# A two-layer trunk in fp32: the first norm's squares added on VectorE, the filter's positions loaded apart, and y stored in four transfers

## The chip, the cores and the metric

The kernel runs on one core of one Trainium2 chip. The metric is device time in microseconds of one execution, the median of several. TensorE's clock has two levels here, 1.2 and 2.4 GHz; the profile gives the granted clock as a share of the upper one.

## What is computed

Two layers over 640 tokens (512 latent, 128 context) of width 1024. Cut to what matters here:

```python
def _rmsnorm(x, w):
    xf = x.astype(jnp.float32)
    y = xf * lax.rsqrt(jnp.mean(xf * xf, axis=-1, keepdims=True) + EPS)
    return (y * w.astype(jnp.float32)).astype(x.dtype)

def _trunk_layer(x, p, l, cond, ctx):
    mod = (cond @ p['w_ada'][l] + p['b_ada'][l]).reshape(cond.shape[0], 1, 6, D_MODEL)
    sh_a, sc_a, gt_a, sh_m, sc_m, gt_m = [mod[:, :, i] for i in range(6)]
    h = _rmsnorm(x, p['norm_mix_w'][l]) * (1.0 + sc_a) + sh_a
    mix, new_ctx = _mixer_sublayer(h, p, l, ctx)
    ...

def _hyena_filters(seq, w1, b1, w2, b2, w3, freq):
    ...
    z = jnp.concatenate([t[:, None], jnp.cos(ang), -jnp.sin(ang)], axis=-1)
    fr = freq.astype(f32)
    h = jnp.sin(fr * (z @ w1.astype(f32) + b1.astype(f32)))
    ...
```

After the two layers a last `_rmsnorm` gives y. The mixer has four branches; the one called Hyena makes its filter from the positions z, which depend on nothing, and applies it by a Fourier transform written as matmuls with tables.

## The kernel before, in words

Everything lies with features on the 128 partitions: x and h are eight chunks (`KC`) of 128 features by 640 tokens (`T`). Every weight is fp32 and comes in blocks of 128x1024 (512 KB) through a ring of four slots, `w_ring`. SP issues the loads in program order; each waits until TensorE has counted the block that had the slot before (`block_done`). ScalarE rounds each block to fp32r (`w_high`, L1744), POOL subtracts it from the weights (`w_low`, L617), and TensorE does three products of high and low parts (L808). All waits are on semaphores written out by hand, and each engine runs its own list in order.

**The start.** SP loads the condition, the first constants and x, and then 16 blocks of `w_early` (L585), in four rounds of four. From each TensorE makes a row block of the modulation: eight thin matmuls of 32 rows (L842; the trace shows two records for each, as for every fp32 matmul of this shape) into a bank of `psA` per round. After each round VectorE copies the rows (L2871), and after the fourth copy the last of four small matmuls turns them (L1688). VectorE adds the bias (`mod`, L2885) and makes the scale `mod_a` (L2157).
Beside this ScalarE squares x chunk by chunk (L1754) into h. After the second round TensorE sums the squares over features, with a matrix of ones, over all eight chunks (`first_norm_sum`, L855). ScalarE takes the root (`rs`, L1767 and L1768), and VectorE scales x into h (`scale_all`, L2181), in its order after the copy of the third round. ScalarE then modulates h (L1776) and rounds it (`h_high`, L1785).
POOL waits for 14 row blocks and issues the rest of the constants and of the parameters (L611, L612), after the 16th the tables (`dft`, L631, 3264 KB), which include the filter's positions `zf`, and then the low parts of the first two weight blocks.

**The entry of a layer.** `first_blocks` runs the first two blocks of the input projection side by side, chunk by chunk as `h_high` comes. Between the high and the low parts stands `filter_first` (L874), four matmuls from `zf`, which waits for `dft_in`. VectorE makes the argument of the sine (L2207 to L2215).

**The end.** `norm_sum(l, at_end)`, root, `scale_all` on VectorE, then ScalarE multiplies each chunk by the last norm's weight (L2146). SP waits for all eight and issues one transfer of y (L600).

The later norms already sum their squares on VectorE (L2821) and leave two chunks to TensorE.

## Time and profile before

| | us |
|---|---|
| median of 3 runs | 2883.03 |
| the three runs | 2883.03, 2883.29, 2879.55 |
| span of the profiled execution | 2881.2 |
| TensorE matmul busy | 2712.8 |
| VectorE busy | 1161.1 |
| ScalarE busy | 858.9 |
| POOL busy | 814.2 |

The profiled execution has no device time of its own beside its span; the span lies among the three runs. The span runs from the first to the last instruction. The page cuts it into 40 slices of 72 us; in the first, TensorE matmuls are busy for 5 tenths, the DMA engines for 8, and the granted clock is 8 tenths, while nearly everywhere after it TensorE is at 8 or 9 and the clock at 9 tenths or more. Shares of busy time are averages; what a stretch is limited by is read from the waits.

### The profile page before, as it was taken

The numbers are of one execution on the slowest core, as the hardware profiler recorded it, in microseconds if no ns is written. First come the engines' busy times: TensorE is split into PE (matmuls) and PEld (weight loads), VectorE is DVE, ScalarE is ACT, GpSimd is POOL, SyncE is SP. The second block draws the span as 40 slices with busy tenths as digits, with TensorE's granted clock in tenths as the row PEclk, the third lists the DMA queues.
The fourth block names the chain that finished last, engine by engine and source line by source line (L and its number), as shares of the span: only waits on it lengthen the run. The fifth ranks groups of instructions, "written<-read, shape, count | busy, mean of one in ns | idle before, by whom it ended". The sixth has DMA issues, their size and how long they took to land.

```text
span 2881.2 us, 56176 instructions
## 1 busy us (share of the span) xinstructions
PE 2712.8 (94%) x24352; PEld 2497.1 (87%) x24352; DVE 1161.1 (40%) x2008; ACT 858.9 (30%) x1326; POOL 814.2 (28%) x525
## 2 busy tenths in 40 slices
PE   5998899999999899999989988999999998999997
PEld 4888887888889899999977887888887998999997
DVE  3666614236633511111375674242565234111113
ACT  3242033333322422122341511433333224122223
POOL 1322121222233233333322311322222332333332
PEclk8999999999999999999999999999999999999999
DMA  8110011221234222222230100112222332222222
GB/s 314 45 48 14 3 46 43 94 83 69 81 108 138 101 88 96 88 96 88 96 135 23 45 4 11 58 68 83 83 81 78 131 102 74 88 95 88 96 88 81
DMA packets 56679, 234.25 MB, mean 81 GB/s; under 512 B 6640, under 2 KB 6800, under 8 KB 55296
## 3 DMA queue, kind: packets, MB, share of 16 engines
q1 hardware_dynamic: 53568, 206.67, 21.3%
q0 software_dynamic: 2880, 24.11, 2.3%
q8 instruction: 193, 3.16, 0.4%
q14 instruction: 38, 0.31, 0.0%
HBM read 221.94 MB, written 8.81 MB: 80 GB/s over the span
## 4 chain that ended last, share of the span: by engine, by line
PE 88%; DVE 6%; ACT 2%; DMA 2%; issue 2%; POOL 0%; SPq 0%; DVEq 0%; POOLq 0%; ACTq 0%
PE ps_dense L808 42%; PE ps_dense L816 15%; PE ps_aux L1457 4%; PE ps_aux L808 4%; PE ps_dense L1410 3%; PE ps_aux L1199 2%; PE ps_dense L1483 1%; PE ps_aux L1410 1%; PE ps_dense L842 1%; PE ps_aux L1185 1%; PE ps_aux L1151 1%; PE ps_dense L1471 1%; DMA w_ring<-in_w_early 1%; DVE arena L2442 1%; PE ps_aux L842 1%
## 5 line engine op out<-in xcount | busy, mean ns | idle before, releaser
L617 POOL TENSOR_TENSOR w_low<-w_ring,w_high 128x1024 fp32r<-128x1024 f32 x256 | 638.9, 2496 | 1317.8 <-ACT w_high L1744 1317.7
L808 PE MATMUL ps_dense<-h_high,w_high 128*128 128x320 f32 x1792 | 422.9, 318 | 38.3 <-ACT h_high L1785 30.4
L1744 ACT ACTIVATE w_high<-w_ring 128x1024 fp32r<-128x1024 f32 x256 | 270.6, 1057 | 553.6 <-PE ps_dense L808 352.3
L808 PE MATMUL ps_dense<-h_low,w_high 128*128 128x320 f32 x1792 | 402.8, 312 | 0.0
L808 PEld LDWEIGHTS ps_dense<-h_high,w_high 128*128 128x128 f32 x1792 | 305.7, 193 | 53.0 <-issue 37.6
L808 PEld LDWEIGHTS ps_dense<-h_low,w_high 128*128 128x128 f32 x1792 | 302.2, 191 | 0.5 <-issue 0.5
L808 PE MATMUL ps_dense<-h_high,w_low 128*128 128x320 f32 x1792 | 295.0, 312 | 0.0
L808 PEld LDWEIGHTS ps_dense<-h_high,w_low 128*128 128x128 f32 x1792 | 274.5, 191 | 0.0
L816 PE MATMUL ps_dense<-h_high,w_high 128*128 128x320 f32 x1024 | 242.5, 318 | 12.7 <-DVE rs L2633 5.8
L808 PE MATMUL ps_dense<-z_high,w_high 128*128 128x320 f32 x1024 | 235.5, 311 | 0.0
L816 PE MATMUL ps_dense<-h_high,w_low 128*128 128x320 f32 x1024 | 233.6, 309 | 0.0
L808 PE MATMUL ps_dense<-z_low,w_high 128*128 128x320 f32 x1024 | 233.3, 309 | 0.0
L816 PE MATMUL ps_dense<-h_low,w_high 128*128 128x320 f32 x1024 | 233.1, 309 | 0.0
L2774 DVE SCALAR_TENSOR_TENSOR x_res<-ps_dense,mod,x_res 128x320 f32<-128x320 f32 (+2 forms) x192 | 72.6, 434 | 342.6 <-PE ps_dense L808 342.6
L816 PEld LDWEIGHTS ps_dense<-h_high,w_high 128*128 128x128 f32 x1024 | 168.2, 189 | 20.7 <-issue 18.7
L2846 DVE CAST z_high<-flow 128x640 fp32r<-128x640 f32 x64 | 33.9, 529 | 368.2 <-ACT flow L2102 368.2
L808 PEld LDWEIGHTS ps_dense<-z_high,w_high 128*128 128x128 f32 x1024 | 170.3, 188 | 3.2 <-issue 3.2
L816 PEld LDWEIGHTS ps_dense<-h_low,w_high 128*128 128x128 f32 x1024 | 171.6, 188 | 0.0
L816 PEld LDWEIGHTS ps_dense<-h_high,w_low 128*128 128x128 f32 x1024 | 171.5, 188 | 0.0
L808 PEld LDWEIGHTS ps_dense<-z_low,w_high 128*128 128x128 f32 x1024 | 171.1, 188 | 0.0
L808 PE MATMUL ps_dense<-z_high,w_low 128*128 128x320 f32 x1024 | 160.6, 309 | 0.0
L808 PEld LDWEIGHTS ps_dense<-z_high,w_low 128*128 128x128 f32 x1024 | 152.8, 188 | 0.0
(450 smaller groups left out, 3931.1 us busy)
## 6 DMA issues: line engine op xcount, KB each, us to landing
w_ring<-in_w_mlp SPq DMA_DIRECT2D x128, 512.0 KB, 3.5
w_ring<-in_w_gate SPq DMA_DIRECT2D x64, 640.0 KB, 3.8
w_ring<-in_w_late SPq DMA_DIRECT2D x64, 512.0 KB, 4.6
w_ring<-in_w_early SPq DMA_DIRECT2D x48, 512.0 KB, 3.5
w_ring<-in_w_in SPq DMA_DIRECT2D x48, 512.0 KB, 3.5
w_ring<-in_w_out SPq DMA_DIRECT2D x16, 512.0 KB, 3.5
arena<-in_dft POOLq DMA_DIRECT2D x2, 3264.0 KB, 16.4
x_kept<-x_res POOLq DMA_DIRECT2D x2, 2560.0 KB, 12.9
```

The source lines that it names most:

```text
L617: g.tensor_tensor(w_low[:, n % 2], ring[:, slot, 0:KC, :], w_high[:, n % 2].bitcast(F32), ALU.subtract).then_inc(w_low_in.sem, 1)
L808: last = mm(out[:, s, 0:HALF], w_[:, par_, k, :], x_[:, k, s * HALF:(s + 1) * HALF], start=first, stop=final)
L816: last = mm(out[:, s, 0:HALF], w_[:, par_, k, :], x_[:, k, s * HALF:(s + 1) * HALF], start=k == 0 and x_ is x_high and w_ is w_high, stop= ...
L842: last = mm(out[32 * (k % 4):32 * (k % 4) + 32], cond_pad[:, k, at:at + 32], ring[:, slot, k, :], start=j == 0 and k < 4, stop=j == of - 1 ...
L1151: return mm(psA[to, 2 * i, u * 64:(u + 1) * 64], lt[s % 3][rows(r), d, hh, rows(r)], mv, start=True, stop=True)
L1185: return mm(psA[rows(r), 2 * i, u * 64:(u + 1) * 64], xt[i][at, u], wm[i][at, u], start=True, stop=True)
L1199: last = mm(out, wm[i][at, u], mv, start=not moved, stop=True)
L1410: last = mm(out[:, s, 0:HALF], w_[:, k, :], x_[:, k, s * HALF:(s + 1) * HALF], start=n == 0 and k == 0, stop=n == 2 and k == 1)
L1457: last = mm(out[:, a:b], qt, k[:, a:b], start=True, stop=True)
L1744: a(w_high[:, n % 2], ring[:, j, 0:KC, :], ACT.Copy).then_inc(w_high_in.sem, 1)
L2774: last = v.scalar_tensor_tensor(out=dst[:, p:q], in0=ps, scalar=gate[:, s:s + 1], in1=dst[:, p:q], op0=ALU.mult, op1=ALU.add)
L2846: v.tensor_copy(z_high[:, j], hid_sq[:, j % 2]).then_inc(hid_high.sem, 1)
```

## The change

Six edits:

1. `first_norm_sum` is one chunk. VectorE adds the squares of chunk c−1 to those of chunk c, for c from 1 to 7, each addition waiting for ScalarE's square and for the addition before; `squares_summed` counts them, and TensorE waits for seven.
2. TensorE does this sum after the second block of the second round, where before it did it after the fourth.
3. VectorE scales x after the copy of the second round, before the third.
4. The positions have a transfer of their own. In layer 0 POOL issues it right after the first part of the parameters, in layer 1 ahead of the tables. `filter_first` waits for that alone; the tables are waited for by VectorE before the first window product, after the fourth convolution.
5. In layer 0 the low parts of the first two weight blocks are made in four pieces of two chunks each.
6. At the end VectorE multiplies by the weight and the root in one step (`scalar_tensor_tensor`), ScalarE's part is gone, and SP issues four transfers of two chunks each.

```diff
         squares_in = signal("squares_summed", 2 * (KC - 2), KC - 1)
...
-            sp.wait_ge(y_ready.sem, KC)
-            sp.dma_start(outs["y"], h[:]).then_inc(y_out.sem, 16)
-            sp.wait_ge(y_out.sem, 16)
+            for c in range(0, KC, 2):
+                sp.wait_ge(*x_scaled.nth(DEPTH, c + 2))
+                sp.dma_start(outs["y"][:, c:c + 2], h[:, c:c + 2]).then_inc(y_out.sem, 16)
+            sp.wait_ge(y_out.sem, KC // 2 * 16)
...
             pool.dma_start(par[:, 0:PAR_FIRST], ins["par"][DEPTH - 1][:, 0:PAR_FIRST]).then_inc(params_in.sem, 16)
+            pool.dma_start(zf, ins["dft"][0:33, at_z:DFT_W]).then_inc(z_in.sem, 16)
             held(pool, block_done.sem, RING + N_EARLY - 2)
...
-                g.tensor_tensor(w_low[:, n % 2], ring[:, slot, 0:KC, :], w_high[:, n % 2].bitcast(F32),
-                                ALU.subtract).then_inc(w_low_in.sem, 1)
+                step = 2 if l == 0 and n < 2 else KC
+                for k in range(0, KC, step):
+                    last = g.tensor_tensor(w_low[:, n % 2, k:k + step], ring[:, slot, k:k + step, :],
+                                           w_high[:, n % 2, k:k + step].bitcast(F32), ALU.subtract)
+                last.then_inc(w_low_in.sem, 1)
...
-                pool.dma_start(dft, ins["dft"]).then_inc(dft_in.sem, 16)
+                if l:
+                    pool.dma_start(zf, ins["dft"][0:33, at_z:DFT_W]).then_inc(z_in.sem, 16)
+                pool.dma_start(dft[:, 0:at_z], ins["dft"][:, 0:at_z]).then_inc(dft_in.sem, 16)
...
             def first_norm_sum():
-                for c in range(KC):
-                    pe.wait_ge(*x_squared.nth(0, c + 1))
-                    for a, b in SEGS:
-                        last = mm(psD[:, 0, a:b], c_("ones"), h[:, c, a:b], start=c == 0, stop=c == KC - 1)
+                pe.wait_ge(squares_in.sem, KC - 1)
+                for a, b in SEGS:
+                    last = mm(psD[:, 0, a:b], c_("ones"), h[:, KC - 1, a:b], start=True, stop=True)
...
-                pe.wait_ge(*dft_in.nth(l, 1))
+                pe.wait_ge(*z_in.nth(l, 1))
...
-                if i == 1:
-                    pe.wait_ge(const_in.sem, 16)
-                    first_norm_sum()
+                    if i == 1 and j == 1:
+                        pe.wait_ge(const_in.sem, 16)
+                        first_norm_sum()
...
-            for c in range(KC):
-                act.wait_ge(*x_scaled.nth(DEPTH, c + 1))
-                a(h[:, c], h[:, c], ACT.Identity, scale=c_("fin")[:, c:c + 1]).then_inc(y_ready.sem, 1)
...
                 if l == DEPTH:
-                    scale_all()
+                    for c in range(KC):
+                        v.scalar_tensor_tensor(out=h[:, c], in0=x[:, c], scalar=c_("fin")[:, c:c + 1], in1=rs[:],
+                                               op0=ALU.mult, op1=ALU.mult).then_inc(x_scaled.sem, 1)
                     return
...
-                dve.wait_ge(*dft_in.nth(l, 1))
                 sin_arg(l, 1, flat, p_("hb1", r), r)
...
                         dve.wait_ge(*x_out.nth(l, 1))
+                        dve.wait_ge(*dft_in.nth(l, 1))
...
+            for c in range(1, KC):
+                dve.wait_ge(*x_squared.nth(0, c + 1))
+                if c > 1:
+                    dve.wait_ge(squares_in.sem, c - 1)
+                v.tensor_tensor(h[:, c], h[:, c], h[:, c - 1], ALU.add).then_inc(squares_in.sem, 1)
             for i in range(N_EARLY // RING):
                 dve.wait_ge(block_done.sem, RING + (i + 1) * RING)
                 v.tensor_copy(first_rows[:, i * P:(i + 1) * P], psA[:, i, 0:P]).then_inc(first_rows_in.sem, 1)
-                if i == 2:
+                if i == 1:
```

How the order moves on TensorE at the start: a row block is eight of the matmuls into `ps_aux`, and the sum is the pairs into `ps_dense` from `h_norm` (640 tokens, in 512 and 128). Before, the end of the eight pairs and what follows; the first eight row blocks (64 matmuls) stand ahead of them:

```order
L855 MATMUL ps_dense<-h_norm,con 128x512
L855 MATMUL ps_dense<-h_norm,con 128x128
L842 MATMUL ps_aux<-w_ring,cond_pad 32x128 x64
L1688 MATMUL ps_aux<-con,bout 128x8 x4
L808 MATMUL ps_dense<-h_high,w_high 128x320 x2
```

Now, from the first matmul on:

```order
L851 MATMUL ps_aux<-w_ring,cond_pad 32x128 x48
L863 MATMUL ps_dense<-h_norm,con 128x512
L863 MATMUL ps_dense<-h_norm,con 128x128
L851 MATMUL ps_aux<-w_ring,cond_pad 32x128 x80
L1696 MATMUL ps_aux<-con,bout 128x8 x4
L817 MATMUL ps_dense<-h_high,w_high 128x320 x2
```

One pair is left of eight, and it stands behind six row blocks (48 matmuls) and ahead of ten (80), where the eight pairs stood behind eight and ahead of eight.

On VectorE, the same part of the program. `cond_pad` is the condition laid out for the row blocks, `bout` takes the copied rows. Before:

```order
L2867 TENSOR_SCALAR cond_pad<-cond_t 128x8x2
L2871 COPY bout<-ps_aux 128x128 x3
L2181 TENSOR_TENSOR h_norm<-x_res,rs 128x640 x8
L2871 COPY bout<-ps_aux 128x128
L2882 MEMSET stage 128x2
L2883 MEMSET stage 128x2x2
L2885 TENSOR_TENSOR mod<-ps_aux,par 128x32
L2157 SCALAR_TENSOR_TENSOR mod_a<-mod,par 128x16
```

Now:

```order
L2874 TENSOR_SCALAR cond_pad<-cond_t 128x8x2
L2880 TENSOR_TENSOR h_norm<-h_norm 128x640 x7
L2883 COPY bout<-ps_aux 128x128 x2
L2188 TENSOR_TENSOR h_norm<-x_res,rs 128x640 x8
L2883 COPY bout<-ps_aux 128x128 x2
L2893 MEMSET stage 128x2
L2894 MEMSET stage 128x2x2
L2896 TENSOR_TENSOR mod<-ps_aux,par 128x32
L2162 SCALAR_TENSOR_TENSOR mod_a<-mod,par 128x16
```

Seven additions stand ahead of the first copy, and the scaling has moved from behind the third copy to behind the second.

## Rows read from the trace of the kernel before

**Rows 1.** The page of the profile: span, and the chain's shares by engine.

```profile
span 2881.2 us, 56176 instructions
...
PE 88%; DVE 6%; ACT 2%; DMA 2%; issue 2%; POOL 0%; SPq 0%; DVEq 0%; POOLq 0%; ACTq 0%
```

**Rows 2.** The chain of waits, 0 to 120 us: start us, us, what.

```profile
17.09 5.70 DMA w_ring<-in_w_early
...
23.92 10.40 PE ps_dense L855 x32
...
36.88 7.14 DMA w_ring<-in_w_early
...
45.77 21.70 DMA arena<-in_dft
```

**Rows 3.** Windows: stretch, busy us of each engine, PEclk, DMA share, GB/s.

```profile
28.00:29.00 1.00, 1.00 (x5) 0.60 (x4) 0.00 (x0) 0.00 (x0) 0.00 (x0) 1.00 0.05 20
50.50:65.30 14.80, 12.05 (x64) 11.28 (x64) 7.68 (x10) 11.17 (x15) 2.88 (x2) 0.76 1.03 416
67.60:76.70 9.10, 9.09 (x37) 7.79 (x37) 5.54 (x9) 2.42 (x5) 0.58 (x1) 0.62 0.58 226
1476.70:1482.00 5.30, 5.30 (x33) 4.54 (x33) 3.70 (x6) 1.38 (x4) 0.00 (x0) 1.00 0.10 6
```

**Rows 4.** Timeline of the start: start us, us, engine, line, operation, idle before.

```profile
10.66 5.12 ACT L1754 ACTIVATE h_norm<-x_res 128x640 f32<-128x640 f32 x8 [8.06 <-DMA x_res<-in_x]
...
19.33 0.65 PE L842 MATMUL ps_aux<-w_ring,cond_pad 128*32 128x128 f32 x16 [1.67 <-DMA w_ring<-in_w_early]
...
21.49 1.08 PE L842 MATMUL ps_aux<-w_ring,cond_pad 128*32 128x128 f32 x16 [1.51 <-DMA w_ring<-in_w_early]
...
37.31 5.97 DVE L2181 TENSOR_TENSOR h_norm<-x_res,rs 128x640 f32<-128x640 f32 x8 [0.74 <-ACT rs L1768]
...
47.29 1.51 DVE L2157 SCALAR_TENSOR_TENSOR mod_a<-mod,par 128x16 f32<-128x16 f32 x1
48.83 0.81 ACT L1776 ACTIVATE h_norm<-h_norm,mod,mod_a 128x512 f32<-128x512 f32 x1 [2.51 <-DVE mod_a L2157]
```

**Rows 5.** SP's timeline, 13 to 14.3 us: the first load of the ring's second round.

```profile
13.35 0.33 SPq L585 DMA_DIRECT2D w_ring<-in_w_early  x1
```

**Rows 6.** POOL's timeline; the page's DMA issues (KB each, us to landing).

```profile
43.87 0.54 POOL L612 DMA_DIRECT2D par<-in_par  x1
...
46.40 2.35 POOL L617 TENSOR_TENSOR w_low<-w_ring,w_high 128x1024 fp32r<-128x1024 f32 x1
...
par<-in_par POOLq DMA_DIRECT2D x1, 1699.0 KB, 13.6
```

**Rows 7.** Timeline of TensorE at the filter's entry, layer 0 and layer 1.

```profile
67.61 1.99 PE L874 MATMUL ps_aux<-arena,par 33*64 33x512 f32 x4 [2.18 <-DMA arena<-in_dft]
...
69.53 7.33 PE L808 MATMUL ps_dense<-h_low,w_high 128*128 128x320 f32 x32
...
1476.70 1.29 PE L874 MATMUL ps_aux<-arena,par 33*64 33x512 f32 x4
...
1477.92 4.95 PE L808 MATMUL ps_dense<-h_low,w_high 128*128 128x320 f32 x32
```

**Rows 8.** Timeline of the end; DMA issues of comparable sizes (KB, us to landing).

```profile
2866.46 5.97 DVE L2181 TENSOR_TENSOR h_norm<-x_res,rs 128x640 f32<-128x640 f32 x8 [5.08 <-ACT rs L1768]
...
2873.32 0.35 SPq L600 DMA_DIRECT2D out_y<-h_norm  x1
...
w_ring<-in_w_gate SPq DMA_DIRECT2D x64, 640.0 KB, 3.8
...
out_y<-h_norm SPq DMA_DIRECT2D x1, 2560.0 KB, 7.4
...
out_state<-bout POOLq DMA_DIRECT2D x2, 128.0 KB, 2.1
```

**Rows 9.** Line 2821, additions of two tiles: duration ns min/median/max.

```profile
L2821 DVE TENSOR_TENSOR h_norm<-h_norm x24: 824/2353/2356, 933.5 to 2854.9; 128x640 f32<-128x640 f32 x24
```

More of the change, by code:

```diff
@@ L247, in trunk @@
         zf = table("z")[0:33]
+        at_z = DFT["z"][0]
+        assert at_z + DFT["z"][1] == DFT_W
         at_win = DFT["win"][0]
```

5 lines of the change are left out of this document (2 added, 3 removed).

## The prediction

> **What bounds the kernel now.** I read the page first. TensorE is 88% of the chain that ended last [rows 1], so a microsecond counts only where TensorE waits for something else. The change touches three such places: the start, the entry to layer 0, and the end. For the first two I read the chain of waits in order of time [rows 2]. The reader should see that up to 69 us it hardly holds dense work: it holds a wait for a weight load that ends at 22.79, 10.40 us of TensorE on the first norm's sum, a wait of 7.14 us for the last row weights, and 21.70 us of the transfer of the filter tables, after which the filter's first matmul starts at 67.6. The windows show what the 10.40 us cost [rows 3]: between 28 and 29 us the DMA engines are 5% busy. All four ring slots hold loaded weights, and TensorE, which alone frees them, is in the norm. Then I read the timeline of the start [rows 4], SP's issues [rows 5], POOL's work and its transfers [rows 6], the filter's entry in both layers [rows 7] and the end [rows 8].
>
> The sum below is made against this execution's span of 2881.2 us [rows 1]; the median of the runs, 2883.0, is 1.8 above it and the lowest run 1.7 below it. I subtract from the median. A measurement of this kernel can tell about 0.2%, 5.8 us, from no change.
>
> **Term 1, the ring streams on.** Now TensorE runs 16 row blocks with the norm's eight chunks after the eighth. The change leaves one chunk and puts it after the sixth. Eight chunks took 10.40 us [rows 2], so one is 1.3 us. The sixth block ends at 19.33 + 0.65 = 19.98 [rows 4]; the chunk then lies in TensorE's wait for the seventh block, which lands at about 21.5, and costs nothing at 1.3 us and about 0.5 at half clock. It needs VectorE's seven additions. ScalarE squares at 0.64 us a chunk from 10.66 [rows 4], so the second square is there at 11.9; an addition of two 128x640 tiles takes 0.82 us alone [rows 9], 0.87 with its wait for the one before, so seven end at 18.0, 2 us before they are wanted. What stands behind them on VectorE is the copy of the first four rows, for which nobody waits until the sixteenth block.
> The root follows about 3 us after the sum, near 25, and the scaling takes 5.97 us [rows 4], to 31: it is put before the third copy, still ahead of the last block.
> When does the last block come? A round of four loads took 22.79 − 13.35 = 9.4 us from its first issue to its last landing [rows 2, 5]. Block eight is done at 23.92 [rows 2]; block nine takes 1.1, so the last round starts at 25.1, lands by 34.5, and the last block ends at 35.7 instead of 45.15 (44.02 and the same 1.1). That gains 9.5; less 0.3 for the chunk at low clock, **9.2**. Bounds: 10.4, the whole sum; and 8.2, if the last load, issued at 28.7, takes the 7.14 us of [rows 2].
>
> **Term 2, the low parts in pieces.** The scale `mod_a` is 16 columns wide and took 1.51 us, ending when POOL's 2.35 us piece ended [rows 4, 6]. ScalarE starts to modulate only then (48.83). Now POOL works in four pieces of some 0.59 us, and VectorE waits for one at most: **0.9**, between 0 and 1.3. POOL's extra starts are covered by ScalarE's first two steps.
>
> **Term 3, the filter's positions apart.** TensorE is idle for 2.18 us before the filter's first matmul, for the table transfer [rows 7]. The positions are 33 rows of 2.5 KB; they now go on POOL's queue at about 11.6 us and are there long before. Next in line is the rest of the parameters, issued at 43.87 with 13.6 to landing, so at 57.5, 8 us before it is wanted [rows 6]; constants and parameters are issued in the new order equally far ahead of the modulation. The tables are wanted by VectorE at the first window product, some 25 us later, and that wait stands beside one for the copied-out x that was there. **2.2**, between 0 and 2.2. In layer 1 the filter's matmuls start with no idle time before them [rows 7], so the split transfer there changes nothing.
>
> **Term 4, the clock behind that wait.** The granted clock was 0.62 in the 9.1 us after it, against 1.00 at the same place of layer 1 [rows 3]; part of the stretch was at 1.2 GHz instead of 2.4. The filter's matmuls took 1.99 against 1.29 us and the 32 of the low part 7.33 against 4.95 [rows 7]. Layer 1 had no wait there. Without the wait layer 0 should be like it: **3.1**, between 0 and 3.1. What is late next is ScalarE's evacuation of the first block and its next weights, about 2 us of work within a low part of 2.3 us for the other block; layer 1 lives with that.
>
> **Term 5, the end.** Now VectorE multiplies by the root from 2866.46 for 5.97 us, ScalarE applies the weight one chunk behind, and one transfer of 2560 KB is issued at 2873.32 and takes 7.4 us [rows 8], to 2880.7. In the change VectorE does both in one step of two tile inputs and a column; the trace has none of this shape from SBUF, and the nearest, the multiplication, runs at 0.75 us apart, or 0.82 if they don't overlap. I take 0.77, near the first since the data are the same: 6.2 us, to 2872.6. Behind the last pair goes one transfer of 640 KB, for which the row of the gate weights has 3.8 us [rows 8]: 2876.4, so **4.3** gained. Bounds: 0.7, if the last quarter still takes 7.4; 6.1, if steps come 0.75 apart and the quarter takes no longer than the 2.1 us of the 128 KB store [rows 8].
> The Trainium skill, DMA: Bandwidth & Descriptors, section Bandwidth, speaks against this part: it advises batches of at least 1 MiB for three quarters of the peak rate, and the quarters are 0.63 MiB. By the fit in its section Anatomy of one DMA an estimate is 8.0 us for the whole and 3.5 for a quarter, which would make term 5 4.6, if only the last quarter shows.
>
> **The sum.** 9.2 + 0.9 + 2.2 + 3.1 + 4.3 = 19.7. 2883.0 − 19.7 = **2863.3 us**.
>
> **Rivals.**
> B. *The filter's entry does not mend.* Another transfer, or ScalarE's last high part, leaves a gap at the same place and the clock falls as before: terms 3 and 4 are gone, 14.4 gained, 2868.6 us. For it: the DMA engines are fully busy up to there, from 50.5 to 65.3 us [rows 3], and x goes out in the same stretch. Against: what the filter needs lands 8 us ahead. Chance 0.12.
> C. *The quarters of y run one behind another.* The first pair is ready at 2868.0; four times 3.8 us gives 2883.2, 2.5 later than now instead of 4.3 earlier: 12.9 gained, 2870.1 us. For it: the four go into one queue. Against: the ring's loads go into one queue too, and four of 512 KB landed within 9.4 us of a first issue though slots came free one by one. Chance 0.05. The skill's rule on batches, in the section named, would point this way.
> D. *VectorE's additions are slow.* The same addition took 2.35 us in most cases where POOL worked [rows 9]. Seven would end at 28.4, and TensorE, with the chunk in its queue ahead of ten row blocks, would stand from 20.0: 8.4 of term 1 lost, 11.3 gained, 2871.7 us. Against: POOL has only two small transfers to issue. Chance 0.04.
> E. *No change that can be told.* B, C and D together leave 19.7 − 5.3 − 6.8 − 8.4 = −0.8: 2883.8 us. Chance 0.03.
> F. *Slower: the clock does not come up in time.* The dense norm sum held the clock at 1.00 from 28 to 29 us [rows 3]. Without it the start is thin row blocks with waits, and the dense blocks of layer 0 might stay at 1.2 GHz. At that level work takes twice its time, so 20 us of full-speed work at half speed eat the gain, and 26 us make it slower by 0.2%. If it lasted to the gate rows, some 45 us of work: 2883.0 + 25 = 2908 us. Against: in the first blocks, 50.5 to 65.3 us, the mean was 0.76 [rows 3], so the clock had fallen before them anyway and came up within them. Chance 0.03. The Trainium skill, TensorE: Matmul & The Clock Gate, section What's actually happening, says that the gate follows how busy the array has recently been; a thinner start would point this way.
>
> **How the numbers follow.** The forecast has the remaining 0.73. Its own upper ends give 23.1, 2859.9 us; the runs before scatter to 3.5 under their median, of which I allow 2.4, so the range starts at 2857.5. Above it takes in B and its scatter and ends at 2870.0; outside lie D to F, most of C and a little scatter, under 0.2. Faster by over 0.2%: the forecast, B, C and D, 0.94. Within 0.2%: E, 0.03. Slower: F, 0.03.
>
> **What would show it.** In the changed profile: a chunk of two norm matmuls near 20 us, with no stretch of idle DMA until the last block, which ends near 35.7 (term 1; D if the chunk starts near 28). `mod_a` at 0.2 to 0.8 us and the modulation starting near 38.7 (term 2). The filter's first matmul directly behind the first blocks, 16.6 us after the modulation's start, with the filter at 1.3 us and the low part at about 5 (terms 3, 4; B if there is a wait, F if matmuls of 128x320 stay near double time beyond the first blocks). Four y transfers about 1.5 us apart, the last landing under 4 us after its issue (term 5; C if the landings grow). The prediction is wrong if the start gains under 12 or the end under 2 us.

## The result, and the profile after

| | before | after |
|---|---|---|
| median, us | 2883.03 | 2863.28 |
| range of the runs, us | 2874.24 to 2891.03 (5) | 2861.15 to 2864.21 (5) |
| span of the profiled execution, us | 2881.2 | 2861.5 |

The ratio of after to before on record is 0.9917, with a 95% interval of 0.9895 to 0.9939, which leaves out 1. The two medians of the table lie 19.75 us apart, a ratio of 0.9931, inside that interval. The forecast was 2863.3. The profiled execution after was measured at 2863.28 us, 1.8 above its span.

That the number is met to a tenth is luck, as the parts show. I cut both traces at five marks: the start of the matmuls that turn the last rows (L1688, now L1696), ScalarE's first modulation, the filter's first matmul (L874, now L882), the filter's second layer (L942, now L950), and VectorE's first step of the last scaling. Times in us:

| mark | before | after | gained since the mark before it | forecast |
|---|---|---|---|---|
| rows turned | 45.08 | 37.23 | 7.85 | 9.2 (term 1) |
| first modulation | 48.83 | 40.06 | 0.92 | 0.9 (term 2) |
| filter, first matmul | 67.61 | 57.96 | 0.88 | 2.2 (term 3) |
| filter, second layer | 83.81 | 71.08 | 3.08 | 3.1 (term 4) |
| last scaling | 2866.46 | 2851.69 | 2.04 | 0 |
| end of the span | 2881.2 | 2861.5 | 4.93 | 4.3 (term 5) |

They sum to 19.70. Terms 1 and 3 fell short by 2.7 together, term 5 gave 0.6 more than forecast, and 2.04 us came from the middle of the kernel, where the change only moves layer 1's positions into a transfer of their own.

The chain of waits of the changed kernel, 0 to 120 us, its pieces of the same stretch (start us, us, what), answering to [rows 2]:

```profile
19.05 6.19 DMA w_ring<-in_w_early
...
26.57 4.80 DMA w_ring<-in_w_early
...
32.70 6.38 DMA w_ring<-in_w_in
...
40.24 2.40 POOL w_low L623 x4
...
43.11 3.97 POOL w_low L623 x4
...
47.12 10.91 PE ps_dense L817 x56
58.03 1.22 PE ps_aux L882 x4
```

The 10.40 us of the norm's sum and the 21.70 us of the tables are gone. In their place stand waits for row weights, for the first block of `w_in` (landing at 39.08), and then something new: POOL's low parts, 2.40 and 3.97 us.

Its windows, answering to [rows 3] (stretch, busy us of each engine with counts, PEclk, DMA share, GB/s):

```profile
28.00:30.00 2.00, 1.08 (x16) 0.60 (x16) 2.00 (x4) 0.00 (x0) 0.00 (x0) 0.50 0.91 277
46.00:57.90 11.90, 10.78 (x56) 10.64 (x56) 5.79 (x7) 6.74 (x10) 1.60 (x2) 0.73 1.02 435
47.12:57.96 10.84, 10.84 (x57) 10.64 (x57) 4.67 (x6) 5.65 (x8) 0.48 (x1) 0.75 1.03 439
57.90:64.00 6.10, 6.10 (x38) 5.28 (x38) 4.47 (x7) 2.10 (x5) 0.26 (x1) 1.00 0.80 305
```

Between 28 and 30 us the DMA engines are now 91% busy, where they were at 5%. Behind the first blocks the clock is at 1.00 up to 64 us. The means over the whole of the first blocks look alike, 0.73 against 0.76, but they cover stretches of different length, with and without waits. So compare the same work, the last 28 pairs of dense matmuls ahead of the filter (a pair is one row of x2 in the timeline, and these are the fifth to the 32nd). Now this work starts at 47.12 and takes 10.84 us at a mean clock of 0.75; in the kernel before it took 9.66:

```profile
55.77:65.43 9.66, 9.54 (x57) 9.01 (x56) 5.22 (x7) 7.42 (x11) 0.20 (x1) 0.90 1.03 405
```

A pair of 128x320 matmuls starts 0.53 us after the one ahead at the lower clock and 0.29 at the upper one, and here more of them ran at the lower. So the first blocks lost 1.2 us by the clock in this pair of traces.

The timeline of the start of the changed kernel, answering to [rows 4]:

```profile
12.27 6.41 DVE L2880 TENSOR_TENSOR h_norm<-h_norm 128x640 f32<-128x640 f32 x7 [9.19 <-ACT h_norm L1762]
...
20.00 2.23 PE L863 MATMUL ps_dense<-h_norm,con 128*128 128x512 f32 x4
...
25.21 5.97 DVE L2188 TENSOR_TENSOR h_norm<-x_res,rs 128x640 f32<-128x640 f32 x8 [1.55 <-ACT rs L1776]
...
36.22 1.08 PE L851 MATMUL ps_aux<-w_ring,cond_pad 128*32 128x128 f32 x16 [0.53 <-DMA w_ring<-in_w_early]
...
39.10 1.06 ACT L1752 ACTIVATE w_high<-w_ring 128x1024 fp32r<-128x1024 f32 x1 [13.99 <-DMA w_ring<-in_w_in]
...
39.44 0.18 DVE L2162 SCALAR_TENSOR_TENSOR mod_a<-mod,par 128x16 f32<-128x16 f32 x1
...
40.06 0.80 ACT L1784 ACTIVATE h_norm<-h_norm,mod,mod_a 128x512 f32<-128x512 f32 x1
40.24 6.83 POOL L623 TENSOR_TENSOR w_low<-w_ring,w_high 128x256 fp32r<-128x256 f32 x8 [1.79 <-ACT w_high L1752]
...
43.20 0.90 PE L817 MATMUL ps_dense<-h_high,w_high 128*128 128x320 f32 x2 [4.10 <-POOL w_low L623]
...
47.12 0.90 PE L817 MATMUL ps_dense<-h_high,w_high 128*128 128x320 f32 x2 [1.41 <-POOL w_low L623]
```

VectorE's seven additions end at 18.7. TensorE's chunk starts at 20.0 and takes 2.2 us, where the prediction counted 1.3 at full clock. The root leads to a scaling from 25.2 to 31.2. `mod_a` takes 0.18 us. The last three rows are what the forecast missed: POOL works for 6.83 us on the two low parts, and TensorE waits for it at 43.20 (4.10 us idle) and again at 47.12 (1.41 us). These waits stand in place of others. In the kernel before, TensorE waited there for ScalarE, and for longer in sum, 6.17 us against 5.51:

```profile
50.56 0.87 PE L808 MATMUL ps_dense<-h_high,w_high 128*128 128x320 f32 x2 [3.60 <-ACT h_high L1785]
...
54.54 0.90 PE L808 MATMUL ps_dense<-h_high,w_high 128*128 128x320 f32 x2 [2.57 <-ACT h_high L1785]
```

The filter's entry, answering to [rows 7]:

```profile
57.96 1.29 PE L882 MATMUL ps_aux<-arena,par 33*64 33x512 f32 x4
...
59.17 4.95 PE L817 MATMUL ps_dense<-h_low,w_high 128*128 128x320 f32 x32
```

Both have the durations that layer 1 had, to the hundredth.

The end, answering to [rows 8]: the timeline, and the page's DMA issues.

```profile
2851.69 6.46 DVE L2172 SCALAR_TENSOR_TENSOR h_norm<-x_res,con,rs 128x640 f32<-128x640 f32 x8 [5.08 <-ACT rs L1776]
2853.40 5.11 SPq L603 DMA_DIRECT2D out_y<-h_norm  x4
```

```profile
out_y<-h_norm SPq DMA_DIRECT2D x4, 640.0 KB, 2.9
```

The fused steps come 0.81 us apart (6.46 for eight); a quarter of y lands 2.9 us after its issue.

### The profile page after: what moved, and what is told of

The parts are those of the page before. It is cut to its first block, busy times and chain, and to the rows that moved or that the text cites. A ratio compares the mean times of both kernels' runs of the same rounds, so it can differ in the third digit from the quotient of the medians.

```text
span 2861.5 us, 56136 instructions
## 1 busy us (share of the span) xinstructions
PE 2700.7 (94%) x24324; PEld 2487.1 (87%) x24324; DVE 1168.8 (41%) x2015; ACT 853.0 (30%) x1318; POOL 817.3 (29%) x533
## 4 chain that ended last, share of the span: by engine, by line
PE 86%; DVE 7%; ACT 2%; issue 2%; DMA 2%; POOL 1%; SPq 0%; DVEq 0%; ACTq 0%; POOLq 0%
PE ps_dense L817 42%; PE ps_dense L825 15%; PE ps_aux L1465 4%; PE ps_aux L817 4%; PE ps_dense L1418 3%; PE ps_aux L1207 2%; PE ps_dense L1491 1%; PE ps_aux L1193 1%; PE ps_dense L851 1%; PE ps_aux L1418 1%; PE ps_aux L1159 1%; PE ps_dense L1479 1%; DMA w_ring<-in_w_early 1%; POOL w_low L623 1%; PE ps_aux L851 1%
## 5 line engine op out<-in xcount | busy, mean ns | idle before, releaser
L623 POOL TENSOR_TENSOR w_low<-w_ring,w_high 128x1024 fp32r<-128x1024 f32 (+1 forms) x262 | 640.6, 2447 | 1309.6 <-ACT w_high L1752 1309.6
L817 PEld LDWEIGHTS ps_dense<-h_high,w_high 128*128 128x128 f32 x1792 | 305.9, 193 | 52.7 <-issue 34.1
L825 PEld LDWEIGHTS ps_dense<-h_high,w_high 128*128 128x128 f32 x1024 | 167.6, 188 | 20.7 <-issue 18.7
L2853 DVE CAST z_high<-flow 128x640 fp32r<-128x640 f32 x64 | 33.9, 529 | 368.2 <-ACT flow L2110 368.2
```

The source lines that it names most:

```text
L623: last = g.tensor_tensor(w_low[:, n % 2, k:k + step], ring[:, slot, k:k + step, :], w_high[:, n % 2, k:k + step].bitcast(F32), ALU.subtract)
L817: last = mm(out[:, s, 0:HALF], w_[:, par_, k, :], x_[:, k, s * HALF:(s + 1) * HALF], start=first, stop=final)
L825: last = mm(out[:, s, 0:HALF], w_[:, par_, k, :], x_[:, k, s * HALF:(s + 1) * HALF], start=k == 0 and x_ is x_high and w_ is w_high, stop= ...
L2853: v.tensor_copy(z_high[:, j], hid_sq[:, j % 2]).then_inc(hid_high.sem, 1)
```

## The experiments

The traces of all of them were cut at the same marks. The two right-hand columns are the middle (from the filter's second layer to the last scaling) and the end. Each row is one profiled execution; e5 to e8 ran on another chip than the other experiments. e9, e10 and e11 were timed in that one execution only.

| kernel | rows turned | first modulation | filter | second layer | middle | end |
|---|---|---|---|---|---|---|
| before | 45.08 | 48.83 | 67.61 | 83.81 | 2782.7 | 14.74 |
| changed | 37.23 | 40.06 | 57.96 | 71.08 | 2780.6 | 9.81 |
| e1 sum back | 44.51 | 47.33 | 66.33 | 79.45 | 2781.9 | 9.77 |
| e2 low parts whole | 36.33 | 38.65 | 56.46 | 69.58 | 2784.0 | 9.81 |
| e3 positions back | 36.27 | 38.80 | 57.74 | 70.84 | 2792.4 | 9.76 |
| e4 y whole | 36.42 | 39.38 | 57.34 | 70.46 | 2783.4 | 14.31 |
| e5 before, positions apart | 41.80 | 45.56 | 62.79 | 75.91 | 2777.4 | 14.71 |
| e6 whole, positions back | 36.53 | 40.70 | 58.13 | 72.77 | 2794.1 | 9.74 |
| e7 whole, y in eight | 36.37 | 38.79 | 55.41 | 68.53 | 2782.7 | 9.03 |
| e8 changed again | 35.56 | 38.49 | 56.28 | 69.40 | 2789.3 | 9.75 |
| e9 sum after the eighth | 35.21 | 38.13 | 56.70 | 69.82 | 2780.3 | 9.73 |
| e10 scaling back | 36.96 | 39.91 | 58.06 | 71.19 | 2786.0 | 9.80 |
| e11 two steps | 35.79 | 38.75 | 56.04 | 69.16 | 2786.6 | 10.38 |
| e12 low parts behind the scale | 37.53 | 39.75 | 57.28 | 70.40 | 2778.5 | 9.07 |

### e1: the sum back on TensorE

```diff
-                pe.wait_ge(squares_in.sem, KC - 1)
-                for a, b in SEGS:
-                    last = mm(psD[:, 0, a:b], c_("ones"), h[:, KC - 1, a:b], start=True, stop=True)
+                for c in range(KC):
+                    pe.wait_ge(*x_squared.nth(0, c + 1))
+                    for a, b in SEGS:
+                        last = mm(psD[:, 0, a:b], c_("ones"), h[:, c, a:b], start=c == 0, stop=c == KC - 1)
...
-                    if i == 1 and j == 1:
-                        pe.wait_ge(const_in.sem, 16)
-                        first_norm_sum()
+                if i == 1:
+                    pe.wait_ge(const_in.sem, 16)
+                    first_norm_sum()
...
-            for c in range(1, KC):
-                dve.wait_ge(*x_squared.nth(0, c + 1))
-                if c > 1:
-                    dve.wait_ge(squares_in.sem, c - 1)
-                v.tensor_tensor(h[:, c], h[:, c], h[:, c - 1], ALU.add).then_inc(squares_in.sem, 1)
...
-                if i == 1:
+                if i == 2:
```

> The changed kernel with edits 1 to 3 undone: TensorE sums all eight chunks of squares after the eighth row block, VectorE makes no additions and scales x after the third copy. Theory (the ring stood still behind the sum): the DMA engines fall idle from about 28 to 36 us again and the sixteen row blocks end near 45 us instead of 37.3, some 7.9 us later; everything after shifts by that, so the time is about 2871. Rival (the row blocks are limited by the memory anyway, and other edits brought the gain): they end within 3 us of 37.3, the time is about 2865.

Measured: 2873.39 us, 0.9959 (0.9939 to 0.9978) of before. Its timeline and a window of it:

```profile
23.58 10.60 PE L864 MATMUL ps_dense<-h_norm,con 128*128 128x512 f32 x32
...
39.82 0.65 PE L851 MATMUL ps_aux<-w_ring,cond_pad 128*32 128x128 f32 x16 [3.76 <-DMA w_ring<-in_w_early]
```

```profile
28.00:34.00 6.00, 6.00 (x24) 3.35 (x22) 0.00 (x0) 0.00 (x0) 0.00 (x0) 1.00 0.01 4
```

The DMA engines are at 1% from 28 to 34 us and TensorE then waits 3.76 us for loads that could only be issued after the sum. The rows are turned at 44.51, 7.3 us after the changed kernel and 8.1 after the mean of the eleven traces with one chunk (36.4, from 35.2 to 37.5). The theory holds, the rival falls. This trace also shows the rest of the start apart from the ring: with edits 4 and 5, and without 1 to 3, the second filter layer comes 34.9 us after the rows, where before took 38.7.

### e2, e6 and e12: the low parts in pieces

e2, from the changed kernel:

```diff
-                step = 2 if l == 0 and n < 2 else KC
+                step = KC
```

> The changed kernel with edit 5 undone: the low parts of the first two weight blocks are made in one piece each. Theory (the pieces cost more than they bring, since each gives VectorE a turn and TensorE waits for the last of them): POOL has both done some 2 us sooner, near 45 instead of 47.1 us, mod_a stays under 0.3 us because POOL starts only at 40.2, and the filter's first matmul comes 1 to 1.5 us sooner than 57.96, the time is about 2862. Rival (the pieces pay, as the prediction had it): mod_a or the first modulation is 0.9 us or more later and the filter's first matmul comes at 58.5 or after, the time is about 2864.

Measured: 2864.73 us, 0.992 (0.9892 to 0.9948). Its timeline:

```profile
38.44 0.17 DVE L2162 SCALAR_TENSOR_TENSOR mod_a<-mod,par 128x16 f32<-128x16 f32 x1
38.62 2.34 POOL L623 TENSOR_TENSOR w_low<-w_ring,w_high 128x1024 fp32r<-128x1024 f32 x1 [1.07 <-ACT w_high L1752]
38.66 2.39 DVE L2180 TENSOR_SCALAR h_norm<-h_norm,mod_a,mod 128x128 f32<-128x128 f32 x1
...
42.02 0.87 PE L817 MATMUL ps_dense<-h_high,w_high 128*128 128x320 f32 x2 [3.91 <-ACT h_high L1793]
...
42.73 1.06 ACT L1752 ACTIVATE w_high<-w_ring 128x1024 fp32r<-128x1024 f32 x1 [0.85 <-DMA w_ring<-in_w_in]
...
43.86 2.36 POOL L623 TENSOR_TENSOR w_low<-w_ring,w_high 128x1024 fp32r<-128x1024 f32 x1 [2.90 <-ACT w_high L1752]
...
45.31 0.90 PE L817 MATMUL ps_dense<-h_high,w_high 128*128 128x320 f32 x2 [1.89 <-ACT h_high L1793]
...
46.54 0.73 PE L817 MATMUL ps_dense<-h_high,w_high 128*128 128x320 f32 x2
```

The row at 38.66 stems from a narrower window of the same timeline. POOL has the second low part at 46.2, 7.6 us after it began the first (the theory had 45), and each takes 2.3 us; TensorE's two waits are now for ScalarE's `h_high`. The filter starts 1.5 us sooner than in the changed kernel, as the theory said, but 0.9 of this is rows turned sooner: from the rows to the filter it is 20.13 against 20.73, and the clock came up sooner as well. In the changed kernel the second group of four pieces took 3.97 us, in e3 and e4 3.36. A piece took 0.72 us at the least and 1.32 at the most, with VectorE steps of 0.82 us beside it; that the pieces wait for turns of VectorE is how I read this, and no run here tests it alone.

What the pieces cost shows at the start of the second weight block's products, the fifth pair of TensorE's dense matmuls, and it is best measured from ScalarE's rounding of that block (`w_high`). In e2 this is 42.73 to 46.54, 3.81 us. The same in e8, which has the pieces:

```profile
41.97 1.06 ACT L1752 ACTIVATE w_high<-w_ring 128x1024 fp32r<-128x1024 f32 x1 [1.91 <-DMA w_ring<-in_w_in]
...
43.10 3.37 POOL L623 TENSOR_TENSOR w_low<-w_ring,w_high 128x256 fp32r<-128x256 f32 x4 [1.62 <-ACT w_high L1752]
...
46.52 0.90 PE L817 MATMUL ps_dense<-h_high,w_high 128*128 128x320 f32 x2 [0.54 <-POOL w_low L623]
```

That is 4.55 us. With pieces it is 4.55 or 4.56 in seven traces (e1, e3, e4, e8 to e11), with whole low parts 3.81 or 3.82 in five (before, e2, e5, e6, e12): pieces cost 0.74 us there. In the two traces where the second block had landed before ScalarE wanted it, it is 5.58 with pieces (changed) and 4.07 whole (e7), 1.5 us.

e6 undoes edit 4 as well (the diff is that of e3 below).

> The changed kernel with edits 4 and 5 undone. In the changed kernel with edit 4 alone undone the tables landed just as the filter wanted them, since the pieces had made the first blocks 1.5 us longer. With whole low parts the filter wants them near 56.2 us and they land near 58. Theory (the clock goes down behind a wait of TensorE of 1.5 to 2 us): a wait of that size, then the four matmuls and the low part partly at the lower clock, and from the modulation's start to the second filter matmul 34 us or more, where whole low parts with positions apart took 30.9. Rival (a wait this short leaves the clock up): 32.5 to 33 us.

Measured: 2871.54 us, 0.9958 (0.9941 to 0.9975). Its timeline:

```profile
38.30 2.33 POOL L622 TENSOR_TENSOR w_low<-w_ring,w_high 128x1024 fp32r<-128x1024 f32 x1 [0.54 <-ACT w_high L1749]
...
38.75 1.92 DVE L2159 SCALAR_TENSOR_TENSOR mod_a<-mod,par 128x16 f32<-128x16 f32 x1
```

```profile
58.13 1.26 PE L879 MATMUL ps_aux<-arena,par 33*64 33x512 f32 x4 [1.69 <-DMA arena<-in_dft]
59.32 6.49 PE L814 MATMUL ps_dense<-h_low,w_high 128*128 128x320 f32 x32
```

Here the first weight block landed sooner, POOL started 0.45 us ahead of VectorE's scale, and `mod_a` took 1.92 us until POOL was done. The modulation came 4.2 us after the rows. So a race between one weight load and one small VectorE step decides when the modulation starts. It decides next to nothing for TensorE. Where `mod_a` slips in ahead of POOL, as in e2, the VectorE step behind it is the one that stands: 2.39 us for a 128x128 step that takes 0.34 alone, and ScalarE's first `h_high` waits 1.67 us for it. TensorE's first dense matmul came 5.90 us after the rows in e6 and 5.69 in e2, and the second block's products 10.21 in both. The pieces cut the loss of `mod_a` itself to about 0.5 us (it took 0.57 in e1, 0.67 in e9, 0.71 in e10) and pay for it with longer low parts.

This agrees with the Trainium skill, SBUF — State Buffer, section SBUF: two separate sides, which states that a VectorE operation with two SBUF inputs and a GpSimd operation that reads SBUF exclude each other for a whole instruction. `mod_a` has two SBUF inputs; the step just ahead of it, which reads PSUM and SBUF, took 0.19 us under a running POOL in the kernel before. The step that took 2.39 us in e2 has one tile input only and stood as long; what is cited here speaks of two.

From the rows to the second filter layer, whole low parts with the positions apart took 33.3 (e2), 32.2 (e7) and, with the collision, 34.1 (e5). With pieces it was 33.9, 34.9, 34.0, 33.8, 34.6, 34.2 and 33.4 (changed, e1, e4, e8, e9, e10, e11). These figures hold the clock too: the last 28 pairs took 9.9 us in e2, 9.5 in e7, 10.4 in e5 and 9.8 to 11.0 with pieces. e12 is e7 with the order fixed:

```diff
+                if l == 0:
+                    pool.wait_ge(*mod_ready.nth(l, 1))
                 for n in range(2):
                     low_part(l, n, n)
```

> Whole low parts and eight transfers of y again, and in layer 0 POOL waits for the modulation's scale before its first low part. With whole low parts the scale took 0.17 us where POOL started behind it (twice) and 1.92 where POOL started 0.45 us ahead of it (once). Theory (with the order fixed both the collision and the pieces' cost are gone): the modulation starts 2.3 us after the turned rows begin, never 4; from the turned rows to the second filter matmul at most 33.3 us, where the pieces had 33.4 to 34.9; last scaling to the end 9.0. Rival (POOL's later start delays TensorE's first low product by as much): 34 us or more.

Measured: 2862.92 us, 0.993 (0.9915 to 0.9944). The modulation came 2.2 us after the rows, the second filter layer 32.9, the end 9.07. The theory's numbers hold in this trace, but it is no test of the fixed order: the first weight block was late there (`w_high` made `w_low` wait anyway), so the new wait had nothing to do in the execution that the profile shows. The second block's products started 10.16 us after the rows, as in e2 and e6; the 0.4 us that the mark is ahead of e2 came behind that, with the clock.

### e3 and e5: the positions apart

e3, from the changed kernel:

```diff
-            pool.dma_start(zf, ins["dft"][0:33, at_z:DFT_W]).then_inc(z_in.sem, 16)
...
-                if l:
-                    pool.dma_start(zf, ins["dft"][0:33, at_z:DFT_W]).then_inc(z_in.sem, 16)
-                pool.dma_start(dft[:, 0:at_z], ins["dft"][:, 0:at_z]).then_inc(dft_in.sem, 16)
+                pool.dma_start(dft, ins["dft"]).then_inc(dft_in.sem, 16)
...
-                pe.wait_ge(*z_in.nth(l, 1))
+                pe.wait_ge(*dft_in.nth(l, 1))
```

> The changed kernel with edit 4 undone: the positions come with the tables in one transfer, and the filter's first matmul waits for it. The tables land near 59.5 us, so the wait is about 1.6 us. Theory (the clock falls behind the wait, and that costs more than the wait): the granted clock is near 0.6 in the 9 us after it, the four matmuls take 2.0 us and the low part 7.3, and the mark at the second filter matmul (71.08 in the changed kernel) comes 4.7 us later; the time is about 2868. Rival (an idle stretch this short does not lower the clock): only the wait is lost, the mark comes 1.6 us later, the time is about 2865.

Measured: 2866.04 us, 0.9921 (0.9895 to 0.9947). Neither came true: the filter started at 57.74 with no wait that the timeline shows, took 1.26 us, and the second layer came at 70.84. The tables had landed just in time, because the first blocks ended late, 21.5 us after the rows where e6 below has 19.9. Of these 1.6 us the pieces are 0.7, a later second weight block 0.5 and the clock 0.3. In the presence of edit 5, edit 4 brought nothing in this trace. That is why e6 undid both. There TensorE waited 1.69 us for the tables, and its low part took 6.49 us against 4.95. The windows behind it:

```profile
55.00:60.00 5.00, 3.31 (x18) 2.31 (x18) 0.66 (x2) 0.00 (x0) 0.00 (x0) 0.99 0.98 417
60.00:65.00 5.00, 5.00 (x26) 5.00 (x25) 4.10 (x7) 1.44 (x4) 0.00 (x0) 0.67 0.62 233
```

The clock fell behind a wait of 1.69 us (0.67 from 60 to 65 us), so the rival's reason fell. But it cost 1.5 us, not 3.1: how much of the work behind a wait runs at the lower level differs between executions. The time from the modulation to the second layer was 32.07, below the 34 of the theory and also below the 32.5 of the rival: the modulation itself came 1.9 us late by the collision, and the first blocks did not follow it.

e5 is edit 4 alone, on the kernel before (the diff is e3's, with the signs turned, and the wait for the tables moved on VectorE).

> The kernel before with edit 4 alone: the filter's positions apart, nothing else changed. The marks of the kernel before: filter's first matmul 67.61 us, second filter matmul 83.81. Theory (the wait for the tables and the lower clock behind it are one cost, and removing the wait removes both): the first filter matmul comes at about 65.4 with no wait, its four take 1.3 us, the low part 4.95, and from the modulation's start to the second mark it is 29.7 us instead of 35.0, 5.3 less; the time is 5 us under the kernel before on the same chip. Rival (the clock falls there anyway, since the first blocks before it ran with gaps): 2.2 less only.

Measured: 2882.15 us, 0.9985 (0.9967 to 1.0002). By the marks it does what was expected: the filter starts with no wait, 17.23 us after the modulation where before took 18.78, the low part takes 4.95, and from the modulation to the second layer it is 30.35 instead of 34.98, 4.6 less. The 0.7 us missing from the expected 5.3 lie ahead of the filter, where the last 28 pairs took 10.37 us for 9.66 by a clock that came up later. From the filter's first matmul to its second layer it is 13.12 us, and so it is, within 0.02, in all twelve traces without a wait there; with the wait it was 16.20 (before) and 14.64 (e6). This is the evidence that the clock behind the wait is a cost of the wait. The whole time does not resolve it; 5 us is inside its interval, and so is nothing.

### e4, e7 and e11: the end

e4 puts y into one transfer:

```diff
-            for c in range(0, KC, 2):
-                sp.wait_ge(*x_scaled.nth(DEPTH, c + 2))
-                sp.dma_start(outs["y"][:, c:c + 2], h[:, c:c + 2]).then_inc(y_out.sem, 16)
-            sp.wait_ge(y_out.sem, KC // 2 * 16)
+            sp.wait_ge(*x_scaled.nth(DEPTH, KC))
+            sp.dma_start(outs["y"], h[:]).then_inc(y_out.sem, 16)
+            sp.wait_ge(y_out.sem, 16)
```

> The changed kernel with y in one transfer of 2560 KB, behind the one-step scaling. From the first step of the last scaling to the end of the span the changed kernel takes 9.81 us and the one before 14.74. Theory (four transfers of 640 KB hide all but the last): here it is 6.5 for the steps and 7.4 to 7.6 for the transfer, some 14.0 us, so of the 4.93 us gained at the end 4.2 are the transfers and 0.7 the step ScalarE no longer makes; the time is about 2867.5. Rival (the fused step gives most of it): under 12.5 us, the time is under 2866.

Measured: 2869.66 us, 0.9942 (0.9921 to 0.9964); the end took 14.31 us against 9.81. Its timeline:

```profile
2853.89 6.46 DVE L2171 SCALAR_TENSOR_TENSOR h_norm<-x_res,con,rs 128x640 f32<-128x640 f32 x8 [5.08 <-ACT rs L1775]
2860.38 0.35 SPq L602 DMA_DIRECT2D out_y<-h_norm  x1
```

The transfers are 4.5 us of the 4.9, the step 0.4. e11 takes only the fused step back:

```diff
...
-                    for c in range(KC):
-                        v.scalar_tensor_tensor(out=h[:, c], in0=x[:, c], scalar=c_("fin")[:, c:c + 1], in1=rs[:],
-                                               op0=ALU.mult, op1=ALU.mult).then_inc(x_scaled.sem, 1)
+                    scale_all()
...
+            for c in range(KC):
+                act.wait_ge(*x_scaled.nth(DEPTH, c + 1))
+                a(h[:, c], h[:, c], ACT.Identity, scale=c_("fin")[:, c:c + 1]).then_inc(y_ready.sem, 1)
```

> The changed kernel with the end in two steps again, VectorE multiplying and ScalarE applying the weight, but y in four transfers. From VectorE's first step to the end of the span the changed kernel takes 9.81 us. Theory (the fused step runs 0.81 apart, the plain multiplication 0.75, and ScalarE trails by 0.87): 5.97 + 0.87 + 0.05 + 2.9 = 9.8 us, the same, so the fused step by itself gives nothing and the transfers all. Rival (ScalarE's step in the path costs its whole 0.83): 10.5 us or more.

Measured, in one execution: 2867.91 us; the end took 10.38 us, between the two and nearer to the rival. So the theory that the fused step gives nothing fails: it is worth 0.57 by this trace and 0.43 by e4's. ScalarE's trailing 0.87, less the 0.49 that eight slower VectorE steps add, and a landing of 3.0 for 2.9, give 0.5. e7 has whole low parts and eight transfers:

```diff
-            for c in range(0, KC, 2):
-                sp.wait_ge(*x_scaled.nth(DEPTH, c + 2))
-                sp.dma_start(outs["y"][:, c:c + 2], h[:, c:c + 2]).then_inc(y_out.sem, 16)
-            sp.wait_ge(y_out.sem, KC // 2 * 16)
+            for c in range(KC):
+                sp.wait_ge(*x_scaled.nth(DEPTH, c + 1))
+                sp.dma_start(outs["y"][:, c:c + 1], h[:, c:c + 1]).then_inc(y_out.sem, 16)
+            sp.wait_ge(y_out.sem, KC * 16)
```

> The version meant to beat both: the changed kernel with whole low parts and y in eight transfers of 320 KB. Theory: from the modulation's start to the second filter matmul 31.0 us as with whole low parts before, where the pieces had 31.0 to 32.1 (end 1.5 us sooner than the changed kernel where the low parts start together); from the first step of the last scaling to the end of the span 9.3 us instead of 9.81, since 320 KB land in about 2.4. In all up to 2 us under the changed kernel, which the whole time can hardly tell, since in the middle of the kernel traces differ by up to 12 us. Rival (eight transfers cost SP's issues, 0.35 us each, and landings grow): the end takes 9.8 us or more.

Measured: 2861.00 us (2857.74 to 2867.99), 0.9922 (0.9904 to 0.9941). From the modulation to the second filter layer it was 29.74 us, 1.3 under what was expected; the last 28 pairs took 9.47, the least of all traces. The end took 9.03 us, and e12's 9.07:

```profile
out_y<-h_norm SPq DMA_DIRECT2D x8, 320.0 KB, 2.2
```

320 KB land in 2.2 us. The gain of 0.75 stands in two traces; the whole time can't show it.

### e8: the changed kernel again

> The changed kernel once more, on the chip of the others of this call, as the measure for them. Theory (its first 71 us and its last 10 repeat, and what differs between executions lies between): second filter matmul within 1.5 us of 71.08, last scaling to the end 9.8 within 0.1, and the stretch between them anywhere from 2780 to 2792 us, longer by half of the time that its records show at the lower clock. Rival (start or end scatter as much as the middle): the marks are off by more than 3 us.

Measured: 2866.02 us (2864.36 to 2875.02), 0.994 (0.9922 to 0.9959), on the chip of e7. The end repeats (9.75); the second layer came at 69.40, 1.7 sooner, a little outside what was expected; the middle is 8.6 us longer than in the first trace. Between e7 and e8 the medians differ by 5 us, of which the start gives 0.9 and the end 0.7 in their traces; their intervals overlap, so it is not shown that e7 or e12 beats the changed kernel.

### e9 and e10: edits 2 and 3

e9 moves the one chunk behind the eighth row block:

```diff
-                    if i == 1 and j == 1:
-                        pe.wait_ge(const_in.sem, 16)
-                        first_norm_sum()
+                if i == 1:
+                    pe.wait_ge(const_in.sem, 16)
+                    first_norm_sum()
```

> The changed kernel with edit 2 undone alone: the one chunk is summed after the eighth row block, not after the sixth. Theory (the place matters little once the sum is one chunk, since TensorE waits 2 us for the ninth block anyway): the chunk starts near 24 us, the sixteenth row block ends at most 1 us later than 37.3, and the end of the scaling, near 35, is still ahead of it. Rival (the place is what frees the ring): the row blocks end 2 us or more later.

Measured, in one execution: 2861.67 us; rows turned at 35.21, the soonest of all. Its chunk:

```profile
23.03 1.35 PE L863 MATMUL ps_dense<-h_norm,con 128*128 128x512 f32 x4
...
25.29 0.64 PE L851 MATMUL ps_aux<-w_ring,cond_pad 128*32 128x128 f32 x16 [0.34 <-DMA w_ring<-in_w_early]
```

The rival falls; the place gives nothing that can be seen. e10 moves the scaling behind the third copy:

```diff
-                if i == 1:
+                if i == 2:
```

> The changed kernel with edit 3 undone alone: VectorE scales x after the third copy. The third copy can be made at about 30 us, so the scaling runs from there to 36, just ahead of the sixteenth row block. Theory: no more than 0.3 us later at the modulation's start. Rival (the copies are what the turned rows wait for): 1 us or more.

Measured, in one execution: 2868.78 us; scaling from 30.68 to 36.6, rows turned at 36.96, modulation 2.95 us later (2.83 in the changed kernel). As the theory said: it is just not late.

## Why the prediction was right, and where it was not

**Term 1, right, 9.2 against 7.85** in the pair of traces, and 7.4 to 8.7 if means are used: with the whole sum the rows were turned at 45.08, 44.51 and 41.80 (mean 43.8), with one chunk at 36.4. e5's 41.80 has a sum of 8.92 us where before had 10.40, since the clock was up. The mechanism is shown by e1. What was sized too large is the start of the last round of loads: the estimate took the ninth block to be there when the eighth was done, at 23.92, so that the round would start at 25.1. TensorE waited for the ninth block until 25.28, and the round started at 26.4, 1.3 us later; it then took 9.8 us, near the 9.4 of the estimate. That edits 2 and 3 matter was implied and is not so: the additions on VectorE carry the term.

**Term 2, right in number at its mark, but not a gain for TensorE.** `mod_a` fell from 1.51 to 0.18, but what starts the modulation now is ScalarE, which makes `w_high` from a late weight block until 40.16. And the 0.92 did not reach TensorE: its first dense matmul came 5.48 us after the rows in the kernel before and 5.97 now. The collision of one VectorE step with POOL costs TensorE nearly nothing, as e6 and e2 show.

**Term 3, too large: 0.88 of 2.2.** The wait of 2.18 us for the tables went, as forecast. The sign given for it, the filter 16.6 us after the modulation's start, was missed by 1.3 us, and two steps of the prediction failed there. The larger is one that it put at nothing: the first blocks were taken to run at the clock that they had before. From the modulation to the second block's products it was 7.06 us against 6.94; the last 28 pairs behind it took 10.84 against 9.66, with TensorE busy for all of the 10.84 and for 9.54 of the 9.66. These 1.18 us are the lower clock, which lasted longer (a mean of 0.75 against 0.90). Why it did stays open; it is not that the dense sum is missing, since with the sum in e1 the same pairs took 11.04, and in e8, the changed kernel again, 9.76. The other step is "POOL's extra starts are covered by ScalarE's first two steps". Eight pieces took 6.83 us instead of twice 2.35, and TensorE waited for them at 43.20 and 47.12. The second weight block was rounded 2.6 us sooner after the rows than before, and the pieces took most of that, so that its products started only 0.8 sooner. e5, where edit 4 is alone, has 1.55 of gain in this stretch and 4.6 up to the second layer.

**Term 4, right: 3.1** in the pair of traces, with both durations as in layer 1. e6 shows how far it can vary: a wait of 1.69 us cost 1.5 by the clock, so 3.1 was this trace's value and not a constant.

**Term 5, 4.93 for 4.3.** The fused steps took 6.46 us for the 6.2 counted, and the quarter landed in 2.9; the row of the gate weights, 3.8, was the wrong neighbour. The y row itself would have been nearer: a store from an idle queue, 7.4 for four times the data. The Trainium skill's fit, which it gives for transfers issued by GpSimd while these are SP's, made an estimate of 3.5 for a quarter, too long as well; its advice on batches of 1 MiB did not bind here, since what counts at the end is the last transfer alone, and e7's eight were better still.

**The middle, 2.04 us that nobody forecast.** Nothing shows it to be the change: e8, the changed kernel again, has a middle 8.6 us longer than the first trace. Over 14 traces the middle is from 2777.4 to 2794.1 us long. I summed, over windows of 10 us from 90 to 2850 us, the time at the lower clock, as 2 × (1 − PEclk) × 10. It goes from 71 (changed) through 85 (before), 102 (e3) to 109 us (e6). A line through the 14 pairs has a slope of 0.44 us per us and leaves 1.2 us of scatter (r = 0.97). The changed trace lies farthest off it, 2.7 us above: the line would give it 6.0 us over the kernel before, and it got 2.04, so the line explains the spread and not this one figure. One place where the clock differs, by the same eight matmuls in e3 and in the changed kernel:

```profile
148.98 3.78 PE L1030 MATMUL ps_aux<-arena 128*128 128x256 f32 x8
```

```profile
149.15 1.99 PE L1033 MATMUL ps_aux<-arena 128*128 128x256 f32 x8
```

The edits leave the program untouched there. From 145 to 156 us the granted clock was 0.50 in e3 and 1.00 in the changed kernel, and the next stretch of dense matmuls began at 162.55 and 156.34, though e3 had been 0.2 us ahead at the filter's second layer. This fits the spread of 17 us among the runs before, and it is why a term of 1 or 2 us can be seen between marks and not in the whole time. Ahead of the filter, not even between marks: the clock there moved the mark by up to 1.6 us.

Of the rivals, B (the entry does not mend) happened in none of the eleven traces that have edit 4: no wait stood before the filter, and the clock did not fall behind it. C fell with landings of 2.9 us, D with additions of 0.82 us that started 0.93 apart (seven in 6.41), E with the result. F, as priced, fell with the clock at 1.00 behind the first blocks; a small piece of what it names, the lower clock lasting longer within them, is the 1.18 us of term 3, without the cause that F gave for it.

## What to carry to other kernels

A small reduction on TensorE in the middle of a stream stops the stream if the same engine frees the buffers: look for a stretch with idle DMA engines and full slots, and put the sum on an engine that waits. Cut an instruction into pieces only where what it blocks is on the path and what waits for its last piece is not; whether ordering the small step first would be cheaper, no run here could show. Follow a gain to the engine that bounds the kernel: counted from the turned rows, the modulation here started 0.9 us sooner and TensorE's dense work 0.5 later. And before a lost microsecond is put down to a wait, compare the stretch that has none. Write the output of the last step out as it is made: the end then costs one small landing. Measure such edits between marks of two traces, with a repeat of one of them, before believing a median.

## What the runs showed of the hardware

- 2560 KB of y landed 7.4 us after its issue, a quarter in 2.9 to 3.0, an eighth in 2.2, with issues some 1.6 us (quarters) and 0.8 us (eighths) apart.
- POOL's 128x1024 subtraction took 2.34 us alone; the same in four pieces of 128x256 took 2.4 to 2.8 in the first group and 3.36 to 3.97 where VectorE had two-input steps of 0.82 us to do between them. Whole, it took 2.91 at such a place (e7).
- A 16-column VectorE step with two SBUF inputs took 0.17 us, or 1.5 to 1.9 us when POOL had begun its 2.35 us step ahead of it. A 128x128 step with one tile input took 0.34 us, or 2.34 to 2.39 when POOL had just begun (e2, e7).
- The granted clock was 1.00 during a TensorE wait of 1.69 us (e6) and of 2.18 us (before) and 0.50 soon behind it, from 60 to 62 us in e6 and from 68 to 74 us in the kernel before; the cost was 1.5 and 3.1 us.
- The same 28 pairs of matmuls, with next to no wait among them, took 9.47 to 11.04 us in the 14 traces, by how soon the clock came up (a mean of 0.87 in e7, of 0.75 in the changed kernel). What decides that stays open.
- The clock also falls in the middle of the kernel at places that differ from one execution to the next. Why it does at one place and not at another stays open; no experiment here was made for it.
